# Two pairs' last gates copied on chip, and a first turn of the expert loop without gathered rows

## The reference, cut to what matters

```python
q = (hf @ w_query).reshape(T, N_PEER_HEADS, 2, PEER_KEY_DIM // 2)
s = jnp.einsum('thpk,hpnk->thpn', q, sub_keys)
s1, i1 = lax.top_k(s[:, :, 0], PEER_TOPK)          # 16 of 128, likewise s2, i2
top_s, pos = lax.top_k(cand, PEER_TOPK)            # 16 of 256 sums, per head
g = jax.nn.softmax(top_s, axis=-1)
a = jax.nn.gelu(jnp.einsum('tkd,td->tk', expert_u[ix], hx), approximate=False)
out = jnp.einsum('tk,tkd->td', gx * a, expert_v[ix])
```

## Time and profile before

| | us |
|---|---|
| median of 3 runs (lowest to highest) | 1818.26 (1815.53 to 1819.26) |
| the profiled execution | 1815.94 |
| its span, first to last instruction | 1813.9 |
| PE / DVE / POOL / ACT busy | 1665.3 / 1506.1 / 916.1 / 645.6 |
| loop: first gate product (L1441) to the last | 719.2 to 1781.7 |

### The profile page before, as it was taken

How to read it: one execution, slowest core, us unless ns; L and a number is a source line. 1 busy time by engine, 2 the same in 40 slices (tenths; PEclk the granted TensorE clock), 3 DMA queues, 4 the chain that set the end, 5 groups by cost and what they waited for, 6 DMA issues and landing times.

```text
span 1813.9 us, 28223 instructions
## 1 busy us (share of the span) xinstructions
PE 1665.3 (92%) x9322; PEld 1442.0 (79%) x9338; DVE 1506.1 (83%) x3069; ACT 645.6 (36%) x1085; POOL 916.1 (51%) x771
## 2 busy tenths in 40 slices
PE   4999998999954886899999999999999999999994
PEld 2776766479953886799999999999999999999993
DVE  0732266457999999799999999999999999999997
ACT  1212266121103785233333333333333333333331
POOL 1101000013402665777778877777666666666661
PEclk9999999999976998999999999999999999999997
DMA  9445202140010668999999999999999999999993
GB/s 355 173 163 208 75 1 98 42 184 3 1 47 1 187 186 253 385 406 409 407 408 390 402 409 409 409 409 409 409 408 409 409 409 403 410 409 407 406 397 124
DMA packets 198137, 518.28 MB, mean 286 GB/s; under 512 B 14643, under 2 KB 64435, under 8 KB 197941
## 3 DMA queue, kind: packets, MB, share of 16 engines
q0 software_dynamic: 73728, 268.47, 37.3%
q1 hardware_dynamic: 122320, 245.59, 36.3%
q10 hardware_dynamic: 2022, 3.38, 0.5%
HBM read 486.45 MB, written 30.93 MB: 285 GB/s over the span
## 4 chain that ended last, share of the span: by engine, by line
PE 79%; DVE 10%; DMA 5%; issue 3%; ACT 3%; POOL 0%; SPq 0%; POOLq 0%; ACTq 0%; DVEq 0%; PEldq 0%; another core or an unknown queue 0%
PE ps L1786 20%; PE ps L1785 20%; PE ps L1784 19%; PE ps L1758 4%; PE ps L1873 4%; DMA arena_w<-in_w_mod 2%; PE ps L1599 2%; PE ps L1603 2%; PE ps L1600 2%; PE ps L1697 2%; DMA arena_w<-in_w_in 1%; ACT arena_w L867 1%; DVE arena L1470 1%; PE ps L1721 1%; DVE arena L1307 1%
## 5 line engine op out<-in xcount | busy, mean ns | idle before, releaser
L1786 PE MATMUL ps<-hT_hi,U_lo 128*128 128x384 f32 x1024 | 344.3, 336 | 0.0
L1784 PE MATMUL ps<-hT_hi,U_hi 128*128 128x384 f32 x1024 | 344.1, 336 | 0.0
L1785 PE MATMUL ps<-hT_lo,U_hi 128*128 128x384 f32 x1024 | 343.5, 335 | 0.0
L537 POOL DMA_INDIRECT rows_under<-in_expert_u,idxn x192 | 273.8, 1426 | 116.4 <-issue 41.8
L1784 PE MATMUL ps<-hT_hi,C_hi 128*128 128x512 f32 x768 | 301.2, 392 | 14.5 <-DVE C_lo L1447 14.5
L537 POOL DMA_INDIRECT rows_under<-in_expert_v,idxn x192 | 242.7, 1264 | 140.4 <-DVE arena L1470 77.8
L1786 PE MATMUL ps<-hT_hi,C_lo 128*128 128x512 f32 x768 | 303.2, 395 | 0.0
L1785 PE MATMUL ps<-hT_lo,C_hi 128*128 128x512 f32 x768 | 303.1, 395 | 0.0
L1470 DVE SCALAR_TENSOR_TENSOR arena<-rows_under,dots,arena 128x1024 f32<-128x1024 f32 x192 | 247.8, 1291 | 4.8
L930 ACT ACTIVATE act_t<-ps 128x384 f32<-128x384 f32 x128 | 63.0, 492 | 386.2 <-PE ps L1786 386.2
L1784 PEld LDWEIGHTS ps<-hT_hi,U_hi 128*128 128x128 f32 x1024 | 192.6, 188 | 4.9
(11 more groups left out here) (273 smaller groups left out, 3010.9 us busy)
## 6 DMA issues: line engine op xcount, KB each, us to landing
U_in<-in_expert_uT SPq DMA_DIRECT2D x128, 512.0 KB, 8.7
arena<-in_expert_v SPq DMA_DIRECT2D x128, 512.0 KB, 6.5
arena_w<-in_w_mod SPq DMA_DIRECT2D x12, 2048.0 KB, 12.4
gate_in<-gates_scratch SPq DMA_DIRECT2D x62, 384.0 KB, 7.9
gates_scratch<-arena_w SPq DMA_DIRECT2D x5, 4096.0 KB, 16.6
arena_w<-in_w_in SPq DMA_DIRECT2D x4, 2048.0 KB, 8.7
arena_w<-in_w_query SPq DMA_DIRECT2D x4, 2048.0 KB, 10.8
arena_w<-in_w_out SPq DMA_DIRECT2D x2, 2048.0 KB, 8.4
```

The costliest lines, as they stand in the source:

```text
L537: pool.indirect_dma_start(out=rowr[row], out_offset=None, in_=table, in_offset=bass.IndirectOffsetOnAxis(ap=idxn[:, g, row:row + 1], axis= ...
L1784: nc.tensor.matmul(out, hi, rhi, start=start, stop=False)
L1785: nc.tensor.matmul(out, hi, rlo, start=False, stop=False)
L1786: return nc.tensor.matmul(out, lo, rhi, start=False, stop=stop)
```

## The change

1. Block 3's gates no longer travel through DRAM for the first two pairs. ACT reads the four chunks of the earlier token blocks ahead (two DMAs behind quad 28 of the last block), and after the last quad copies the last two chunks from `gbuf` to `gate_in` itself (two copies, semaphore `s_gtop`). The two DMAs of the whole 384 KB, and ACT's wait for the written gates, go.
2. POOL's row 0 also waits for these copies; row 2 waits for the first written part (`s_gpart[0]`) and not for the gates read back.
3. DVE's turn 0 has no gathered rows. In their places stand the rest of `choose(4)`: its two one-hot selections behind blocks 0 and 1 and its gate weights behind block 2.
4. Turns 1 to 16 take 17 rows each (rows 0 to 271), written out instead of looped; from turn 17 on all is as before.

```diff
@@ sync
             sp.wait_ge(s_spill, 16 * NBLK)
+            sp.wait_ge(s_gtop, 2)
@@ gpsimd, fetch
                 if first and row == 0:
                     pool.wait_ge(s_gout[0], 16 * NDEN)
+                    pool.wait_ge(s_gtop, 2)
                 if first and row == 2:
-                    for part in s_gin:
-                        pool.wait_ge(part, 16)
+                    pool.wait_ge(s_gpart[0], 16)
@@ scalar, gate phase
+                if b == NDEN and p == QUADS - 4:
+                    act.wait_ge(s_diff, QUADS * NDEN)
+                    for g in range(2):
+                        act.dma_start(gate_in[:, g, 0:4 * P].rearrange("p (c n) -> p c n", c=4),
+                                      gates_d[g, :, 0:4].rearrange("p c e t -> p c (e t)")).then_inc(s_gin[g], 16)
+            act.wait_ge(s_gev, QUADS * NDEN)
+            for g in range(2):
+                act.copy(gate_in[:, g, 4 * P:6 * P].rearrange("p (c e t) -> p c e t", c=2, e=2),
+                         gbuf[:, :, 2 * g:2 * g + 2, :]).then_inc(s_gtop, 1)
             share_exps(NDEN + 1)
-            act.wait_ge(s_gout[0], 16 * NDEN)
-            act.wait_ge(s_gout[1], 16 * (NDEN - 1))
-            act.wait_ge(s_gpart[0], 16)
-            for g in range(2):
-                act.dma_start(gate_in[:, g], gates_d[g].rearrange("p c e t -> p (c e t)")).then_inc(s_gin[g], 16)
@@ vector
-            choose(4, 0, 0, 0, (0, 0))
+            candidates(4, 0, 0)
+            def prompt_choice(i, q):
+                n = 2 * i + q // 4
+                if q % 4 == 3 and n < 2:
+                    picked(4, (n,))
+                elif q % 4 == 3 and n == 2:
+                    gate_weights(4)
+            def behind_row(i, q):
+                r = (i - 2) * RR + q + (i // 2 - 1)
+                one_row(r)
+                if i % 2 and q == RR - 1:
+                    one_row(r + 1)
             for g in range(2):
-                experts(0, g, False, dot_row(0))
-            turns(1, TWICE // 4, dot_row(0))
-            turns(TWICE // 4, TWICE // 2, dot_row(1))
-            coefs(0)
-            dve.wait_ge(s_acc0, 1)
-            turns(TWICE // 2, 3 * TWICE // 4, add_row(0))
+                experts(0, g, False, prompt_choice)
+            for turn in range(1, CAUGHT + 1):
+                for g in range(2):
+                    experts(turn, g, False, behind_row)
+            turns(CAUGHT + 1, 3 * TWICE // 4, add_row(0))
```

More of the change, by code:

```diff
@@ L53 @@
 TWICE = PAIRS // 2
+CAUGHT = 16
 HB = P // 2
@@ L329, in program @@
         s_gq = sem("s_gq"); s_gev = sem("s_gev"); s_gout = [sem(f"s_gout{i}") for i in range(2)]
-        s_gpart = [sem(f"s_gpart{i}") for i in range(len(GCUT) - 1)]; s_acc0 = sem("s_acc0")
+        s_gpart = [sem(f"s_gpart{i}") for i in range(len(GCUT) - 1)]; s_acc0 = sem("s_acc0"); s_gtop = sem("s_gtop")
         s_uin = [sem(f"s_uin{i}") for i in range(2)]
@@ L1324, in key_tops, with select @@
                     pair_last(*paired)
-            def select(n, bd=0, share=(0, 0, 0, 0)):
-                b = ORDER[n]
+            def select(n):
                 link(dve.tensor_copy(gsum[:, 1, :], top[:, n, :, 0]))
@@ L1346, in select, with picked @@
                     dve.wait_ge(s_selfill, min(n, NDEN))
-                for w in range(2):
+            def picked(n, ws, bd=0, share=(0, 0, 0, 0)):
+                b = ORDER[n]
+                for w in ws:
                     gate_quads(bd, share[2 * w])
@@ L1358, in select @@
                                            spread(onehot[:, 1]), ALU.add))
+                if ws[-1] == 0:
+                    return
                 if n < NDEN:
@@ L1388, in gate_rows, with candidates @@
                 ins.then_inc(s_rhs1, 1)
-            def choose(n, bd, pairs_share, select_share, weights_share):
+            def candidates(n, bd, pairs_share):
                 pair_sums(n, 3)
@@ L1399, in choose @@
                 dve.wait_ge(s_step, made[1])
-                select(n, bd, (select_share,) * 4)
+                select(n)
+            def choose(n, bd, pairs_share, select_share, weights_share):
+                candidates(n, bd, pairs_share)
+                picked(n, (0, 1), bd, (select_share,) * 4)
                 gate_quads(bd, weights_share[0])
@@ L1435, in experts @@
                 dve.wait_ge(s_gin[g], 16 * (turn + 1))
+                if isinstance(turn, int) and turn == 0:
+                    dve.wait_ge(s_gtop, g + 1)
                 weights = gate_in[:, g].rearrange("p (c e t) -> p e c t", e=2, t=HB)
@@ L1451, in experts @@
                     row(i, 4 * j + 3)
[L1453 to L1461, removed]
             def add_row(k):
@@ L1477, in coefs, with one_row @@
                 dve.wait_ge(s_coef, k + 1)
+            def one_row(r):
+                k, q = r // SLOTS, r % RR
+                if r == 2 * SLOTS:
+                    coefs(0)
+                    dve.wait_ge(s_acc0, 1)
+                at = slice(r % SLOTS, r % SLOTS + 1)
+                dve.wait_ge(s_row[q], 16 * (r // RR + 1))
+                if k < 2:
+                    dve.scalar_tensor_tensor(out=rowr[q], in0=rowr[q], scalar=1.0, in1=h2row[k], op0=ALU.mult, op1=ALU.mult,
+                                             accum_out=dots[:, k, at]).then_inc(s_used, 1)
+                else:
+                    dve.wait_ge(s_used, r)
+                    dve.scalar_tensor_tensor(out=accS[:, k - 2], in0=rowr[q], scalar=dots[:, k - 2, at], in1=accS[:, k - 2],
+                                             op0=ALU.mult, op1=ALU.add).then_inc(s_used, 1)
+            def behind_row(i, q):
[3 more added lines that the diff above has]
+                    one_row(r + 1)
             def residual(n):
```

## The result

The changed kernel takes 1831.16 us (median of 4 runs, 1829.9 to 1832.42) beside 1818.3 before: a ratio of 1.0071, interval 1.0057 to 1.0085. It is 13 us slower. The forecast was 1813.9, its range ended at 1822.5.

A forecast was written before the change was run, and what follows sets the result against it. PE was taken to bound the loop, DMA engines 1 or 2% behind. Profiled 1815.94 - 4.6 + 0.3 = 1811.6 us, with 2.3 us added for the median: 1813.9; range 1803.5 to 1822.5.

The forecast's parts named there:

- On-chip gates: Handover, before sums_v(0): gates copied on chip start it at 715.5 us, 8.2 us gained, no idle and no slow clock.
- The one gap: Block 2 of turn 0: PE idles 3.6 us before sums_v(2), which starts at 736.5, ended by C_lo.
- U(4): Handover: the next late load, issued by SP at about 717 us and landing at 733.5, bounds 732 and 736.
- DVE has time for a 17th row: Turns 1 to 16: DVE has 1.8 us free in a turn, one row costs 1.23; PE does not see it.
- hidden room: Rival: the DMA engines can exceed 409 GB/s, so the full 14 us gain stays: 1804 us; chance 0.17.
- the slower rival: Idle DMA in turn 0 costs more than the handover gains, deciding at 5 us idle: 1821 to 1824; chance 0.18.
- Turn 1: End of the handover: turn 1 comes at about 745.5 us instead of 760.19, 14.7 us gained, bounds 10 and 17.
- Turns 1 to 16: 17-row turns limited by DMA: 541.1 us, turn 17 starting at 1286.6 against 1291.19, 4.6 us of gain left.
- The rate: Turns 1 to 16: DMA moves 406 GB/s, the mean of these turns in the kernel before.
- The bytes: Turns 1 to 16: 222.3 MB, less 7 rows lying ready, plus two reloads of x: 219.7 MB.
- The signs: Trace of turns 2 to 16: 406 to 409 GB/s, DVE waiting for rows from about turn 6, turns of 33.8 to 34.3 us.
- Behind turn 17: After the 17-row turns: PE leads again; 0.3 us added for row-queue start-up and a dip against DVE's lead.

The follow-up runs named there:

- the rows alone: Changed kernel's empty turn 0, choice in it and 17-row turns, but first gates through DRAM as in the kernel before: 1829.94 us, ratio 1.0058.
- the on-chip gates alone: Kernel before plus on-chip gate copies and POOL's earlier fetches; 16 rows every turn, choice ahead of the loop, write on SP's queue: 1822.01 us, ratio 1.0023.
- the changed kernel with light gate loads: Changed kernel with each gate load of the loop cut from 384 to 64 KB, 17th row kept: 1812.23 us, ratio 0.9976.
- the kernel before with light gate loads: Kernel before with each gate load of the loop cut from 384 to 64 KB: 1817.89 us, ratio 0.9989.
- the narrow one: Changed kernel with DVE's operation on the 17th row cut to 128 of 1024 columns, its DMA whole: 1827.93 us, ratio 1.0059.
- PE cut: Kernel before with the lo x hi products of scores_u and sums_v left out: 1814.22 us, one run.
- the second study of the on-chip gates alone: Kernel before plus on-chip gates and earlier fetches, the 3584 KB gate write on ACT's queue, timed again with more rounds: 1812.94 us, ratio 0.9975.

## Why the prediction was wrong, point by point

The sum was 1811.6 us for the profiled execution, which took 1832.42: 20.8 us more. Of these 4.2 lie in the handover, 12.2 in turns 1 to 16, 1.9 behind them, and 2.5 ahead of the last gate product.

**Right.** On-chip gates: sums_v(0) starts at 717.69, 715.2 if the 2.5 us of earlier stages are taken off, against a forecast 715.5, with no gap and short products (0.39 us). The one gap is before sums_v(2), ended by C_lo, with U(4) the late transfer. DVE has time for a 17th row, within 2 or 3 us. The DMA engines have no hidden room (the slices that read 409 are 11, not 12), and turns 2 to 16 ran at 404 to 409 GB/s in windows of 100 us. The case that came true was the slower rival, idle DMA in turn 0, with the mechanism as stated and a chance of 0.18, but the time given for it, 1821 to 1824, was 7 us short.

**U(4), mis-sized by the one fact that I missed.** I had it issued at about 717. The wait of SP on its own queue, 14.53 us, stood in the sum at nothing: I had counted the write's bytes, not its hold on the queue. It could have been read from the trace of before, from SP's timeline there, 8 us behind a gate write of 4096 KB that took 16.6 us to land:

```profile
692.35 4.68 SPq L416 DMA_DIRECT2D U_in<-in_expert_uT  x1
```

In the kernel before V(3) is issued at 724.83, in 0.48 us, 17 us after the write and 5.5 before it lands. The stalls fit that: the issue goes out 3 us before the write lands in the changed kernel, 4 before in the row above, 5 with the rows alone (where V(3) comes 14 us after the write and stands 3.26) and 8 with the on-chip gates alone. An issue that comes as late as that doesn't stand. U_in was used at 738.12, which is 735.6 without the 2.5 us of earlier stages, instead of 733.5; the gap was 6.48 us instead of 3.6, and the clock that it cost came on top: 0.88 granted between 737 and 765 us, 0.79 us for the first product behind the gap, 0.39 before it. Turn 1 came 10.5 us earlier than before against the gates' end, not 14.7.

**Turns 1 to 16: 553.3 us, predicted 541.1.** This is the step that failed. Two terms of it were wrong. The rate: I took 406 GB/s from the first of these turns on, as if the DMA engines were full by then; over all 16 it was 401, since turn 1 ran at 311. POOL, whose row 7 went out at 743.06, asked for no further row until DVE had freed two, at 756.97:

```profile
743.06 1.01 POOL L539 DMA_INDIRECT arena<-in_expert_u,idxn  x1 [21.75 <-DVE gates L1384]
...
756.97 1.86 POOL L539 DMA_INDIRECT rows_under<-in_expert_u,idxn  x1 [12.52 <-DVE rows_under L1503]
```

219.7 MB at 401 GB/s are 547.9 us, 6.8 more than forecast. The bytes: 553.3 us at 401 are 221.9 MB, 2.2 more than I had after crediting 7 rows that lay ready; 5.5 us. POOL issued 270 rows in these turns where the credit left 265, and x was reloaded three times (at 1032.66, 1136.41 and 1240.98 us), as every third turn from turn 10 on would have it too, where the prediction's sum has two. Together that is the 12.2 us; since both shares are worked out from the measured time, their sum proves nothing by itself.

The more direct sum would have been the bytes of the handover: 25.5 MB instead of 30.9 went through in the 84 us after the last gate product, and 5.4 MB are 13 us at 409 GB/s. For 8.1 of these 84 us no packet was under way at all, 1.3 before. The rival's text had "it decides at 5 us of idle DMA" and took 8 to 11 as its case, which is what came; it erred in pricing that at 3 to 6 us, since it named a rate of 401 as an argument, at 6.8 us, and left it out of its time.

The signs differed in part too. The turns were 33.5 to 34.8 us long from turn 1 on, not from turn 6, PE idled 0.8 us in turns 4 and 5, where I had it never idle, and the waits were ACT's for U_in far more than DVE's for gathered rows (141.3 us and 14.0).

**Behind turn 17: +2.2 us, predicted +0.3.** The other kernels with 17 rows in all of turns 1 to 16 show it too (524.9 to 526.1 us from turn 17 to the end, against 522.7), and the changed kernel with light gate loads does not (522.9), which speaks for a full DMA queue as the cause. But the kernel before with light gate loads has 524.8, so the term stays at the edge of what one execution tells, and its cause is not shown.

**What stays open.** By PE's starts the light kernel leaves 2 of the 19 us, and the narrow one gains 2 to 3, with intervals that overlap: whether some of the loss is DVE's, or the order of work's, was not shown. No run shows either what it is in the queue that makes an issue stand, the bytes of the write or the number of its pieces, nor how large a write, or how much traffic beside it, it takes before the issue behind it stands: V(3) behind the first 1 MB piece went out freely (0.35 us), V(4) behind 2.5 MB stood.

## What to carry to other kernels

Before work is moved from one stage to the next, count the bytes of each stage against the highest rate that the trace ever sustains, here 409 GB/s: when the next stage is at 98% of it, a transfer that the first stage no longer makes is not hidden later but added at full price. A large write, here of 3584 KB in pieces of 512 bytes, belongs on a queue behind which nothing urgent is issued; look in the timeline for an issue of over 1 us. Test the parts of a change apart: here one of them, with its queue put right, was a gain of 0.3% inside a change that lost 0.7%.

## What the runs showed of the hardware

A DMA issue, 0.33 to 0.66 us in a free queue, held its engine for 10.1 to 14.8 us in eight kernels, on SP or on ACT, where a 3584 or 2560 KB write in pieces of 512 bytes stood ahead on that queue (the 10.13 us on ACT are two issues together); POOL's own issues went on meanwhile (0.93 us at 719.13 and 0.94 at 720.37 in the changed kernel). In the kernel before it is 4.68 us behind a write of 4096 KB. I had not expected this of an instruction that only hands over work.

The DMA engines never sustained more than 409 GB/s here: 400 us at 409 with PE cut, 413 over 28 us at best, in the second study of the on-chip gates alone. The Trainium skill, "DMA: Bandwidth & Descriptors", section Bandwidth, gives 425 GB/s for a 16 MB load; no run of this kernel, whose pieces are rows of 4 KB and gates of 512 bytes, comes to it.
